# Gates applied as expert rows leave PSUM, and stored rows added to the residual by DMA

## The reference, cut to what matters

```python
gate = p_grp * p_exp / jnp.sum(p_exp, axis=-1, keepdims=True)
...
def expert_block(args):
    xe, e = args
    hid = jax.nn.silu(xe @ w1[e]) * (xe @ w3[e])
    return hid @ w2[e]

yb = lax.map(expert_block, (xb, blk_e)).reshape(p_tot, d)
out = jnp.zeros((n + 1, d), u.dtype).at[buf_tok].add(yb * buf_w[:, None].astype(yb.dtype))
...
h = h + hier_moe(...)
return rmsnorm(h, norm_final_g)[:, N_META:]
```

## Time and profile before

| | |
|---|---|
| median of 3 runs | 2345.99 us (2345.4 to 2348.33) |
| span of the profiled execution | 2346.7 us |
| TensorE busy | 2189.0 us, 93% |
| VectorE busy | 986.8 us, 42% |
| ScalarE busy | 435.3 us, 19% |
| Pool busy | 102.7 us, 4% |
| DMA | 347.50 MB, mean 148 GB/s |

### The profile page before, as it was taken

How to read it: one execution, slowest core, us unless ns; L and a number is a source line. 1 busy time by engine, 2 the same in 40 slices (tenths; PEclk the granted TensorE clock), 3 DMA queues, 4 the chain that set the end, 5 groups by cost and what they waited for, 6 DMA issues and landing times.

```text
span 2346.7 us, 25276 instructions
## 1 busy us (share of the span) xinstructions
PE 2189.0 (93%) x9706; PEld 1458.3 (62%) x9706; DVE 986.8 (42%) x1990; ACT 435.3 (19%) x819; POOL 102.7 (4%) x136
## 2 busy tenths in 40 slices
PE   8999999999989999999999999998999988777886
PEld 6888888545657788888764566556885432222232
DVE  6455434124776555553443245767651400000014
ACT  2010100145362110100022012552112000000001
POOL 0000000000101000000011000210000010000000
PEclk9999999999999999999999999999999998898998
DMA  5132222311021322232114222000243799999997
GB/s 159 54 105 75 74 97 81 104 36 36 1 90 38 124 90 72 92 110 86 63 45 106 53 54 86 5 12 28 89 134 166 300 424 426 428 427 427 426 394 303
DMA packets 172682, 347.50 MB, mean 148 GB/s; under 512 B 18083, under 2 KB 143139, under 8 KB 152098
## 3 DMA queue, kind: packets, MB, share of 16 engines
q1 hardware_dynamic: 166496, 331.66, 38.1%
q0 software_dynamic: 5504, 12.32, 1.4%
q10 hardware_dynamic: 578, 2.10, 0.2%
HBM read 337.33 MB, written 16.26 MB: 151 GB/s over the span
## 4 chain that ended last, share of the span: by engine, by line
PE 71%; DMA 16%; DVE 5%; issue 3%; ACT 2%; DVEq 1%; SPq 1%; ACTq 0%; POOL 0%; POOLq 0%
PE PS L608 20%; DMA M<-w 11%; PE PS L639 10%; PE PS L3396 7%; PE PS L73 7%; PE PS L2747 5%; DMA M<-w_ffn_up 3%; PE PS L2920 2%; PE PS L388 2%; PE PS L972 2%; PE PS L1546 2%; PE PS L1903 1%; PE PS L942 1%; PE PS L999 1%; DMA M<-expert_rows 1%
## 5 line engine op out<-in xcount | busy, mean ns | idle before, releaser
L608 PE MATMUL PS<-M 128*128 128x256 f32 x2464 | 537.1, 380 | 4.0 <-DMA M<-w_ffn_up 2.2
L608 PEld LDWEIGHTS PS<-M 128*128 128x128 f32 x2464 | 466.5, 190 | 75.2 <-DMA M<-w_ffn_up 9.6
L3396 PE MATMUL PS<-M 128*64 128x512 f32 x1536 | 360.6, 629 | 83.8 <-DMA M<-w 60.7
L3396 PEld LDWEIGHTS PS<-M 128*64 128x64 f32 x1536 | 113.9, 145 | 318.1 <-issue 216.0
L639 PE MATMUL PS<-M 128*128 128x256 f32 x1232 | 268.9, 379 | 5.2 <-DVE M L797 2.7
L639 PEld LDWEIGHTS PS<-M 128*128 128x128 f32 x1232 | 233.4, 190 | 42.5 <-issue 11.2
L3496 DVE TENSOR_TENSOR M<-M,PS 128x512 f32<-128x512 f32 x16 | 11.0, 688 | 409.2 <-PE PS L3396 409.2
L734 DVE TENSOR_TENSOR M<-M,PS 128x256 f32<-128x256 f32 x220 | 92.6, 421 | 199.1 <-PE PS L608 194.7
L73 PE MATMUL PS<-M 128*128 128x264 f32 (+1 forms) x502 | 166.3, 490 | 3.7 <-ACT M L311 1.3
L2747 PE MATMUL PS<-M 128*128 128x256 f32 x616 | 135.1, 380 | 4.0 <-DVE M L2847 2.1
L73 PEld LDWEIGHTS PS<-M 128*128 128x128 f32 x502 | 94.2, 190 | 69.6 <-issue 54.7
(11 more groups left out here) (394 smaller groups left out, 2264.8 us busy)
## 6 DMA issues: line engine op xcount, KB each, us to landing
M<-w SPq DMA_DIRECT2D x128, 1024.0 KB, 18.7
M<-w SPq DMA_DIRECT2D x32, 2048.0 KB, 24.5
M<-w_ffn_gate SPq DMA_DIRECT2D x22, 1024.0 KB, 5.4
M<-w_ffn_up SPq DMA_DIRECT2D x22, 1024.0 KB, 5.3
M<-w_ffn_down SPq DMA_DIRECT2D x16, 1024.0 KB, 5.1
M<-w_in SPq DMA_DIRECT2D x13, 1024.0 KB, 5.3
M<-w_in SPq DMA_DIRECT2D x25, 512.0 KB, 3.8
M<-w_ffn_down SPq DMA_DIRECT2D x8, 768.0 KB, 4.4
```

The costliest lines, as they stand in the source:

```text
L608: last = nc.tensor.matmul(PS[:, 3 * half + BANK[p], 0:HALF], lhs[:, a, :], rhs[:, a, :], start=p in FIRST and a == 0, stop=p in LAST and a ...
L3396: last = nc.tensor.matmul(PS[ROWS * k:ROWS * k + ROWS, bank, :], wide[:, a * P + ROWS * k:a * P + ROWS * k + ROWS], weights(k), start=star ...
```

## The change

Every slot's gate is worked out as its row number is: the product of `BH` with a matrix `AG` that holds the gates (four VectorE operations, eight TensorE products in pair 0 between w1 and w3), copied by ScalarE to `SLOT_GATES`. `rows_out` scales by a column of it as it evicts. `BH` moves by 1024 words, so that it outlives the first `XT_`. The stored rows and the last pair's rows then have their gates, `C10["last"]` becomes 0 or 1, and the four loads by SP and the eight weighted additions on VectorE go. Pool instead issues eight transfers with `accum_op=ALU.add` from `y_dram` onto `HN[:, t, :]`, 512 KB each: first choice for the four tiles, then the second choice for each tile once its first has landed (`comb_in[t]`). VectorE waits for 32 on `comb_in[t]` ahead of its addition from PSUM. Two semaphores are reused from earlier stages, with their counts as offsets.

```diff
--- before.py
+++ after.py
@@ -3053,7 +3053,7 @@
         UN = [at(RG0, D), at(RG0 + 1024, D), at(WORK0, D), at(WORK0 + 13472, D)]
         JUNK = at(HT0, D)
         RW = at(RG0 + 2048, KD, 36)
-        BH = at(RG0, 2, NT * P)
+        BH = at(RG0 + 1024, 2, NT * P)
         CMP = at(RG0 + 2400, 1280)
         AH = at(RG0 + 3700, 2, NT * PAIRS)
         sc0 = [WORK0 + 34976]
@@ -3078,6 +3078,7 @@
         BT, YT, SECOND = small(PAIRS, dt=I32), small(PAIRS, dt=I32), small(PAIRS)
         EBF, EBI, PAIRS_F, PAIRS_I = small(2, SPILL + 1), small(2, SPILL + 1, dt=I32), small(2), small(2, dt=I32)
         IDX, IDY = small(1, dt=I32), small(1, dt=I32)
+        AG, SLOT_GATES = small(2, NT, PAIRS), small(PAIRS)
         CG = [at(base + 2 * D * n, 2, D) for base in (XN0, WORK0 + 8192) for n in range(2)]
         GFIN = GROW
         LAST_SLOTS = [at(HT0 + 2048 + P * n, P) for n in range(2 * NT)]
@@ -3095,8 +3096,8 @@
         g_in, y_st = sems("g_in", "y_st")
         x_tp, x_cp, h_one, h_done, h_silu, h_mul, h_tp, h_cp, y_done, y_cp = sems(
             "x_tp", "x_cp", "h_one", "h_done", "h_silu", "h_mul", "h_tp", "h_cp", "y_done", "y_cp")
-        comb_in, frs, fout = x_in + [sem(f"comb_in{t}") for t in range(2, NT)], sem("frs"), sem("fout")
-        rows_stored, = sems("rows_stored")
+        comb_in, fout = [sem(f"comb_in{t}") for t in range(NT)], sem("fout")
+        frs, FRS0, rows_stored, ROWS_STORED = tails_set, 2, zeroed, 2
         hsum = sem("hsum")
         spare_in, SPARE_IN0 = masks_in, 16 * 6
         U_STORED = 16 * (NT + 1)
@@ -3266,8 +3267,7 @@
             ts_(LAST_PAIR, PAIRS_F[:, 0:1], -1.0, None, ALU.add)
             then(ts_(EBI, EBF, float(EXPERTS - 1), None, ALU.min))
             for j in range(2):
-                stt(C10["last"][:, NT * j:NT * j + NT], C10["pair"][:, NT * j:NT * j + NT], LAST_PAIR, C5[f"ga{j + 1}"],
-                    ALU.is_equal, ALU.mult)
+                ts_(C10["last"][:, NT * j:NT * j + NT], C10["pair"][:, NT * j:NT * j + NT], LAST_PAIR, None, ALU.is_equal)
             dve.drain()
 
 
@@ -3386,6 +3386,13 @@
             scatter_rows(pool, rest + (BASE - 3))
             pool.wait_ge(y_st, rest * 16 + 16 * (BASE - 1))
             pool.sem_inc(rows_stored, 1)
+            pool.wait_ge(rows_stored, ROWS_STORED)
+            for j in range(2):
+                for t in range(NT):
+                    if j == 1:
+                        pool.wait_ge(comb_in[t], 16)
+                    lo = S1 * j + P * t
+                    pool.dma_start(HN[:, t, :], y_dram[lo:lo + P], accum_op=ALU.add).then_inc(comb_in[t], 16)
 
         LAST_BANKS = (0, 2, 5, 0)
 
@@ -3404,13 +3411,23 @@
             def spare_rows(k, a):
                 return SPARE[k][:, a, :] if a < KD // 2 else SPARE[2][:, a - KD // 2, :] if k == 0 else W3B[1][:, a, :]
 
-            def w1_w3(i, c, loaded, third=up_rows):
+            def slot_gates():
+                for j in range(2):
+                    pe.wait_ge(routing_given, 4 + j)
+                    for t in range(NT):
+                        last = nc.tensor.matmul(PS[:, 7, 0:PAIRS], BH[:, j, t * P:(t + 1) * P], AG[:, j, t, :],
+                                                start=j == t == 0, stop=j == 1 and t == NT - 1)
+                last.then_inc(routing_made, 1)
+
+            def w1_w3(i, c, loaded, third=up_rows, between=None):
                 pe.wait_ge(x_cp, i + 1)
                 pe.wait_ge(h_mul, i + 1)
                 pe.wait_ge(w1_in[c], loaded)
                 for a in range(KD):
                     last = both(2, XT_, lambda k: W1B[c][k][:, a, :], a, a == 0, a == KD - 1)
                 last.then_inc(h_one, 1)
+                if between is not None:
+                    between()
                 for a in range(KD):
                     if a % (KD // 2) == 0:
                         pe.wait_ge(w3_in[a * 2 // KD], i * 32 + 32)
@@ -3436,7 +3453,7 @@
             for c in range(2):
                 if c:
                     pe.wait_ge(spare_in, SPARE_IN0 + 48)
-                w1_w3(c, c, 32, spare_rows if c else up_rows)
+                w1_w3(c, c, 32, spare_rows if c else up_rows, None if c else slot_gates)
                 transpose_rows(pe, 16 * c + 32)
                 w2(c)
             with pe.Fori(1, AHEAD // 2) as i:
@@ -3450,7 +3467,7 @@
                 transpose_rows(pe, i * 16 + (16 * AHEAD + 32))
                 w2(i + AHEAD)
             pe_last = pairs_of(pe) - 1
-            pe.wait_ge(routing_given, 4)
+            pe.wait_ge(routing_given, 6)
             for t in range(NT):
                 for j in range(2):
                     last = nc.tensor.matmul(PS[:, 7, P * t:P * t + P], LAST_SLOTS[2 * t + j], ident, start=j == 0, stop=j == 1)
@@ -3471,19 +3488,23 @@
             nc.scalar.preload_act_table_set(SILU)
             pairs = pairs_of(act)
 
-            def rows_out():
-                nc.scalar.activation(YO.rearrange("p (c n) -> p c n", c=2), PS[:, 5:7, :], ACT.Copy).then_inc(y_cp, 1)
+            def rows_out(gate):
+                nc.scalar.activation(YO.rearrange("p (c n) -> p c n", c=2), PS[:, 5:7, :], ACT.Copy,
+                                     scale=gate).then_inc(y_cp, 1)
 
             act.wait_ge(h_one, 1)
             nc.scalar.activation(SG2, PS[:, 2, :], ACT.Silu).then_inc(h_silu, 1)
+            act.wait_ge(routing_made, 3)
+            nc.scalar.activation(SLOT_GATES, PS[:, 7, 0:PAIRS], ACT.Copy)
+            act.drain()
             act.wait_ge(y_done, 1)
-            rows_out()
+            rows_out(SLOT_GATES[:, 0:1])
             with act.Fori(1, pairs) as i:
                 act.wait_ge(h_one, i + 1)
                 nc.scalar.activation(SG2, PS[:, 2, :], ACT.Silu).then_inc(h_silu, 1)
                 act.wait_ge(y_done, i + 1)
                 act.wait_ge(y_st, i * 16 + 16)
-                rows_out()
+                rows_out(SLOT_GATES[:, ds(i, 1)])
 
         def experts_dve(dve):
             def rows_in(n):
@@ -3500,6 +3521,11 @@
                 nc.vector.tensor_copy(HTT, PS[:, 4, :]).then_inc(h_cp, 1)
 
             rows_in(1)
+            for j in range(2):
+                nc.vector.tensor_tensor(AG[:, j], over(C["iota"][:, 0:PAIRS], NT),
+                                        bc(C10["pair"][:, NT * j:NT * j + NT], PAIRS), ALU.is_equal)
+                dve.drain()
+                nc.vector.tensor_tensor(AG[:, j], AG[:, j], bc(C5[f"ga{j + 1}"], PAIRS), ALU.mult).then_inc(routing_given, 1)
             with dve.Fori(0, pairs_of(dve) - 1) as i:
                 hidden(i)
                 rows_in(i + 2)
@@ -3511,7 +3537,7 @@
                     ins = nc.vector.tensor_scalar(LAST_SLOTS[2 * t + j], C["iota"], C10["in"][:, n:n + 1],
                                                   C10["last"][:, n:n + 1], ALU.is_equal, ALU.mult)
             ins.then_inc(routing_given, 1)
-            dve.wait_ge(routing_made, 3)
+            dve.wait_ge(routing_made, 4)
             nc.vector.tensor_copy(LAST_GATES, PS[:, 7, :]).then_inc(last_gates, 1)
             hidden(dve_last)
             turned(dve_last)
@@ -3521,31 +3547,20 @@
             def normed(t):
                 if t == 0:
                     dve.wait_ge(gains_in, 32)
-                dve.wait_ge(frs, t + 1)
+                dve.wait_ge(frs, FRS0 + t + 1)
                 nc.vector.scalar_tensor_tensor(CG[t][:, 0, :], HN[:, t, :], C5["rs"][:, t:t + 1], GFIN,
                                                ALU.mult, ALU.mult).then_inc(fout, 1)
 
-            def weighted(t):
-                dve.wait_ge(comb_in[t], COMB_IN[t])
-                for j in range(2):
-                    nc.vector.scalar_tensor_tensor(HN[:, t, :], CG[t][:, j, :], C5[f"ga{j + 1}"][:, t:t + 1],
-                                                   HN[:, t, :], ALU.mult, ALU.add)
-                    dve.drain()
-
             def last_pair(t):
+                dve.wait_ge(comb_in[t], COMB_IN)
                 dve.wait_ge(last_added, t + 1)
                 row = HN[:, t, :].rearrange("p (c n) -> p c n", c=2)
                 nc.vector.tensor_tensor(row, row, PS[:, LAST_BANKS[t]:LAST_BANKS[t] + 2, :], ALU.add).then_inc(hsum, 1)
 
-            weighted(0)
-            weighted(1)
-            last_pair(0)
-            for t in range(2, NT):
-                weighted(t)
-                last_pair(t - 1)
-                normed(t - 2)
-            last_pair(NT - 1)
-            normed(NT - 2)
+            for t in range(NT):
+                last_pair(t)
+                if t > 0:
+                    normed(t - 1)
             normed(NT - 1)
 
         def final_act(act):
@@ -3559,15 +3574,11 @@
                 nc.scalar.activation(C5["rs"][:, t:t + 1], C5["rs"][:, t:t + 1], ACT.Exp, scale=-0.5).then_inc(frs, 1)
 
         OUT_DMAS = NT
-        COMB_IN = (X_IN[0] + 16, X_IN[1] + 16, 16, 16)
+        COMB_IN = 32
 
         def moe_sp(sp):
             route_sp(sp)
             experts_sp(sp)
-            sp.wait_ge(rows_stored, 1)
```

(4 more changed lines are left out.)

## The result

| | before | changed |
|---|---|---|
| median, first set | 2345.66 us (6 runs) | 2353.31 us (6 runs, 2350.21 to 2355.06) |
| ratio, 95% interval | | 1.0029 (1.0018 to 1.0039) |
| median, second set | 2347.0 us (28 runs) | 2354.36 us (6 runs) |
| ratio, 95% interval | | 1.0033 (1.0021 to 1.0045) |
| span of the profiled execution | 2346.7 us | 2353.2 us |

By the medians the change makes the kernel slower by 7.7 us in the first set and 7.4 us in the second; by the ratios it is 6.8 us (4.2 to 9.1) and 7.7 us (4.9 to 10.6). The forecast was +6.3 us. The listed times of the changed kernel's runs lie 1.8 to 1.9 us over their spans, and the profiled one is the slowest of its six (2355.06), so the two medians compare better than the two spans do; the spans differ by 6.5 us.

The account below looks back on a forecast made before the run. The 16 DMA engines were taken to bound the expert loop and VectorE the tail. 2346.7 - 5.4 + 9.7 + 1.5 + 0.5 = 2353.0 us profiled, 2352.3 us predicted, +0.27%; range 2342 to 2359 us.

Parts of the forecast that it names:

- The bound: Expert loop bound by full DMA engines, tail by VectorE, with about 10 us of its work taken away.
- slack of 0.24 us: Last w2 transfer lands at 2319.9, TensorE loads its weights at 2320.14; any delay there delays TensorE at once.
- Part 1, -5.4 us: VectorE at the end: eight additions of 1.28 us go, TensorE then bounds, norm 3 starts 5.4 us earlier.
- Turns: In the last w2, queues alternate packet by packet; 32 remaining weight packets each wait for one adding packet.
- The sign: TensorE waits about 10 us for weights mid last w2, half clock behind it, sums landing near 2340.
- The price of an adding packet, 0.31 us: Each adding packet in the tail takes 0.31 us, double the plain price of 0.155 us.
- (a): Rival for the last w2: a turn costs 0.155 us, delay 5.0 us, 2347.4 us, no change; chance 0.30.
- (c): Rival for the last w2: the adding packet costs 0.507 us, delay 16.2 us, 2359.1 us; chance 0.12.
- (b): Rival for the tail: adding transfers take no w2 turns that matter, 2341.1 us, faster by 0.2%; chance 0.12.
- The clock, +1.5 us: In the last w2, TensorE's stall lowers its granted clock, costing 1.5 us more.
- Hidden sums: Sums land at 2339.7, before addition 3 would start at 2345.6: hidden by 6 us.
- Part 3, +0.5 us: Gate products in pair 0 delay pair 1's w2 transfers by 2.2 us, partly covered by queued weights: 0.5 us.

Follow-up runs that it names:

- e4: Changed kernel without the four adding transfers of the second choice, those rows left out of the result; executed once, 2353.02 us.
- e5: Changed kernel with only two adding transfers, first choice of tiles 0 and 1, other stored rows left out; executed once, 2349.27 us.
- e2: Changed kernel with Pool's eight transfers as plain loads, all issued at once, and VectorE adding them; 2354.16 us, ratio 1.0031 to before.
- e3: Changed kernel, but Pool waits for the last w2 weights before its first adding transfer; 2355.59 us, ratio 1.0035 to before.
- e8: Changed kernel with filler products on TensorE in the last w2, three ahead of the first half, seven ahead of the second; 2351.50 us, ratio 1.0021.
- the second profile: Profile of the changed kernel run again, with nothing altered; 2354.36 us, ratio 1.0033 to before.
- c4: Changed kernel with adding transfers undone (SP loads the stored rows, VectorE adds) and gates worked out in routing; 2346.57 us, ratio 0.9998 to before.
- e7: Changed kernel with the slots' gates worked out in routing, replacing two filler products there, not in pair 0; 2354.84 us, ratio 1.0038 to before.
- e7b: Repeat of e7: changed kernel with the slots' gates worked out in routing; 2353.11 us, ratio 1.0025 to before.
- e1: Changed kernel with gates at the eviction kept, adding transfers undone: SP loads the stored rows, VectorE adds them; 2347.17 us, ratio 1.0004 to before.
- c3: As c4, but Pool's engine adds the last tile's rows in place of VectorE; 2347.58 us, ratio 1.0001 to before.

## Why the prediction was right

Step by step, in the profile's terms.

- **The bound.** Right: the tail's chain now goes through the weights' landing and TensorE up to the first addition, not through VectorE's weighted additions, and the slack of 0.24 us at the earlier trace rows was the point on which it turned.
- **Part 1, -5.4 us.** From the end of TensorE's last w2 (2324.17 before, 2335.26 after) to the end of the span are 22.5 us before and 17.9 us after: -4.6 us. The order of operations was as worked out. From the first gate product to the last addition are 8.8 us, not 8.5, the eviction and its start take 0.2 us more, and the last store lands 0.3 us later.
- **Turns.** Right, and shown by e4, e5 and e2. Their number was about 27 and not 32. This is an estimate: undelayed, the last data would have ended 22.3 us after the issue at 2298.2 (23.7 less 1.4), which is 8.2 us or 27 weight packets after the first adding packet; no row counts the packets of the late engine alone. That packet moved at 2312.3, 4.0 us after its issue at 2308.25, not 2.6 us as after the zero fill. With full engines the start took longer: 3.8 us in e2 as well, 1.7 us in e3 with idle ones. This is the mis-sized term: 1.4 us late there and 0.1 us in the issue, five turns, 1.6 us of delay (8.2 us for the forecast's 9.9).
- **The sign.** In part wrong. No wait of 10 us stands in the middle of the last w2. The first half's weights are delayed as well, so TensorE waits 3.60 us ahead of the first half (0.78 before), runs it in 6.60 us at the low clock, and waits 3.33 us in the middle. The second half starts at 2330.20, 33.3 us after the first of the four issues, where its first weight load came after 25.3 us before: that is the 8.05 us of delay.
- **The price of an adding packet, 0.31 us.** Right: 0.31 us. No row had shown it; it was chosen by argument between 0.155 and 0.507 us, and the forecast stands or falls with it. It is 1.9 times the plain packet counted in the same way. The Trainium skill's ratio of 1.93 for two reads and one write ("Collectives: The Full Stack"), measured there on collectives, agrees with 209 to 215 GB/s against 407 GB/s for 4 KB loads here. The Trainium skill's rule of packet-wise turns between queues ("DMA: Bandwidth & Descriptors") agrees with 73 to 73 packets in e2. In the Trainium skill such a packet holds several descriptors, and no run here shows whether one packet of the profile is one of those. Rivals (a) and (c) fall with this number, rival (b) with the turns.
- **The clock, +1.5 us.** That it costs time is shown by e8. The size: 5.06 us against 3.65, 1.4 us in the profile; 2.6 us in the second profile, and 2.9 us in the timed medians. That the stall alone causes it is too strong, as e3 and c4 have a low clock there without one.
- **Hidden sums.** Right: the last sums landed near 2341.3 (issue at 2331.6 and 9.7 us), and addition 3 began at 2345.43. No addition waited for them.
- **Part 3, +0.5 us.** Too small in the profile: the loop is 2.5 us longer in it, with pair 0 starting 0.5 us earlier. The cover that was counted on wasn't there: pair 1's w2 transfers go out 2.0 us later in the loop, the first lands in 4.8 us instead of 6.5, and the share falls to 0.55. How much of the 2.5 us this is stays open, since e7 and e7b have loops 1.2 to 1.5 us over before's without gates in pair 0. In timed runs gates alone cost 0.9 us (0.9995 to 1.0014), which the 0.5 us fits.

The tail's terms add up to 4.5 us measured (8.05 for the later start of w2's second half, 1.0 for its longer run counted from its first weight load, 4.6 back), the loop's and what lies before it to 2.0 us: 6.5 us of span. The forecast had 9.7, 1.5, 5.4 back and 0.5. So the path, the turns and the price were right, but that the sum came within 0.2 us of the spans' difference is luck: delay and clock were 2.2 us too high, and the saving and part 3 together 2.3 us too favourable. The timed difference of 7.5 us is about 1 us more; a longer stretch at the low clock, as in the second profile, would give it, but this is argued, not shown.

## What to carry to other kernels

Moving work from an engine that bounds the end to a queue of DMAs moves it beside whatever those DMA engines still carry: ask not whether the transfers fit, but which transfer with no slack takes turns with them. Count the packets that the critical transfer has left and multiply by the price of the other queue's packet. A transfer on the same queue, behind the critical one, cost it nothing here (landings of 23.3 to 23.7 us in before, e1, c3 and c4); the same bytes on another queue cost it a turn for each packet (27.6 us in e2). And a stall of TensorE can be paid twice, in waiting and in the clock behind it, which fillers can save (e8).

## What the runs showed of the hardware

- An adding transfer (4 KB packets, DRAM onto SBUF, single precision) holds the DMA engines 1.9 times as long as a plain load of the same packets: 209 to 215 GB/s against 407 GB/s, 0.31 us a packet.
- Pool's first packet moves 1.7 us after the issue with idle engines (e3), 3.8 to 4.0 us with full ones (e2 and the changed kernel).
- In the last w2, filler products through the stall kept the granted clock at 1.00, and the products behind it took 3.65 us instead of 5.06 to 6.27 us.
- While Pool's engine added two SBUF operands (c3), an addition of two SBUF operands on VectorE took 3.36 us instead of 1.22, its norm 2.08 us instead of 1.28, and its addition from PSUM 1.22 us as ever; the two slow ones ended 1.1 us behind the Pool instruction that ran when they started.
- The granted clock was 0.50 to 0.61 at the start of the last w2 in c4 and e3, behind idle times of TensorE of 0.86 and 0.78 us and without a wait for weights; with the same idle times it was 1.00 in e1 and before.
